# Attention block with keys and values formed once per head and head pairs, and the norms' weights and bias applied by VectorE in two combined steps

## Chip, cores and metric

The kernel runs on one core of one Trainium2 chip. The metric is the device time of one execution in microseconds (us). It is one long program of stages that follow each other with a barrier of all engines between them: a recurrent mixer, a gated feed-forward network (FFN), an attention block, a second FFN, a hybrid mixer and a mixture of experts. The change touches the attention block and the four layer norms that end the first four stages.

## What is computed

Cut from the reference: the attention block picks 128 of up to 512 earlier tokens for each query by a small indexer, and attends over them in 16 heads. Keys and values are both made from one latent of 128 numbers per token.

```
T=512  heads H=16  head width dh=64  latent 128  k_sel=128
proj  = h @ w_in                      # q, latent, q_idx, k_idx, w_idx
ckv   = rmsnorm(proj[..latent..])
score = sum_i w_idx[t,i] * relu(q_idx[t,i] . k_idx[s])      # 8 index heads, causal
sel   = top_k(score, 128)
q_lat[t,h] = q[t,h] @ w_uk[h]         # 64 -> 128
logits     = q_lat . ckv[s] / 8 + rel_bias[bucket(t-s), h]
p          = softmax over s in sel
o_lat[t,h] = sum_s p * ckv[s]
o[t,h]     = o_lat[t,h] @ w_uv[h]     # 128 -> 64
out        = o @ w_out
```

Each of the first two blocks ends its mixer and its FFN with `x = layernorm(ALPHA*x + (1+gate)*y) * g + b`.

## The kernel before, in words

Everything is fp32 with tokens in four tiles `t` of 128 rows. Each engine has its own instruction list, written out by hand, and semaphores order them; nothing is scheduled by a planner, so the order in the code is the order on the engine.

**Attention (`dsa`).** TensorE (PE) transposes `x`, then runs 17 projection jobs of 8 matmuls each (`project`, L1527): 4 for the latent, 1 for `ki`, 4 for `qi`, and after the indexer's scores 8 for the queries `qT`. ScalarE (ACT) copies each result out of PSUM. The scores (L1546) are 24 matmuls with a contraction of 64 rows, even index heads from rows 0 to 63 and odd ones from rows 64 to 127; ACT applies relu, VectorE (DVE) adds them up in `sel` (L1726, L1729), then finds the 128 largest of each row in 16 rounds per tile (L1739, L1740; 48 rounds of growing width) and turns `sel` into 0 or -1e30.

The loop over 16 heads then does for each head `h`: PE projects the query into the latent (`query_latents`, L1591), ACT copies it to `q_lat` (L1670); PE multiplies `q_lat` with `ckvT` for four causal tiles of 128, 256, 384 and 512 columns (L1601); DVE adds the bias (L1757), then adds `sel` and takes the row maximum in one instruction (L1759), and negates it (L1761); ACT takes the exponentials (L1687); PE transposes the ten 128x128 blocks of probabilities (`attend`, L1566); ACT copies them to `PT` (L1682); PE multiplies with `ckv` (`output`, L1576), ACT copies `o_lat` (L1692), PE applies `w_uv` (`project_output`, L1583), and DVE divides by the row sums (`finish`, L1747). The logits of head `h` stand on PE ahead of the transposes of head `h-1`. After the last head PE transposes the output (L1619) and multiplies it with `w_out` (L1626), 16 matmuls per token tile.

**Norms.** `deepnorm_rows` on DVE takes for each tile: gate times PSUM (L435), plus ALPHA times `x` (L436), statistics (L438), each in two halves; mean and variance (L439, L440); it waits for ACT's square root, takes the reciprocal (L442), and scales the tile in one instruction (L443). `affine_rows` on GpSimd (POOL) multiplies by `g` (L451) and adds `b` (L453), and SyncE (SP) stores the tile. It is used four times: in the mixer's last stage (tiles named `mixed_`), in both FFNs (`ffn_`) and in the attention block (`dsa_`, where `y` lies in `dsa_qT`).

Of the kernel before, what the change touches and what calls it, by code (L numbers as in the profile page):

```python
# [98 lines left out]
def swiglu(nc, phase, x_in, mod, w_in, w_out, ln_g, ln_b, ident_dram, x_out, next_cond, next_w, next_b, next_mod):  # L99
# [8 lines left out]
    with ExitStack() as ctx:  # L108
# [8 lines left out]
        with ExitStack() as down_ctx:  # L117
# [24 lines left out]
                   y_psum steps root var_done scaled g_done normed stored wi_highs wi_split wo_highs wo_split act_steps  # L142
# [15 lines left out]
        with nc.Block() as block:  # L158
# [54 lines left out]
            def _(pool):  # L213
# [6 lines left out]
                affine_rows(nc, pool, y, g, b, (s["v_loaded"], 16 * 3), s["scaled"], s["g_done"], s["normed"])  # L220
# [119 lines left out]
            def _(dve):  # L340
# [5 lines left out]
                for b in range(2):  # L346
                    nc.vector.memset(marks[:, 4 + b:5 + b], 0.0).then_inc(nstored[b], 16)
# [72 lines left out]
                for f in range(2, NF):  # L420
# [4 lines left out]
                deepnorm_rows(nc, dve, link, lambda t, j: bank[2 * t + j], s["y_psum"], x_again, gt, y, st, mv, rstd,  # L425
                              s["var_done"], s["root"], s["scaled"])


def deepnorm_rows(nc, dve, link, bank_of, y_psum, x, gt, y, st, mv, rstd, var_done, root, scaled):

    for t in range(NT):
# [11 lines left out]
        nc.vector.tensor_scalar(y[:, t, :], y[:, t, :], mv[:, t, 0:1], rstd[:, t:t + 1], ALU.subtract, ALU.mult).then_inc(scaled, 1)  # L443


def affine_rows(nc, pool, y, g, b, v_loaded, scaled, g_done, normed):

    pool.wait_ge(*v_loaded)
    for t in range(NT):
        pool.wait_ge(scaled, t + 1)  # L450
        nc.gpsimd.tensor_tensor(y[:, t, :], y[:, t, :], g[:, :], ALU.mult).then_inc(g_done, 1)  # L451
        pool.wait_ge(g_done, t + 1)
        nc.gpsimd.tensor_tensor(y[:, t, :], y[:, t, :], b[:, :], ALU.add).then_inc(normed, 1)  # L453

# [736 lines left out]
def rwkv_finish(nc, room, buf, Y, acc, x_in, mod, w, ln_g, ln_b, ident_dram, x_out):  # L1191
# [40 lines left out]
    scaled = room.sem("scaled")  # L1232
    g_done = room.sem("g_done")
# [4 lines left out]
    with nc.Block() as block:  # L1238
# [16 lines left out]
        def _(pool):  # L1255
# [3 lines left out]
            affine_rows(nc, pool, y, g, b, (v_loaded, 16 * 2), scaled, g_done, normed)  # L1259
# [51 lines left out]
        def _(dve):  # L1311
# [26 lines left out]
            deepnorm_rows(nc, dve, link, lambda t, j: bank[2 * (t % 3) + j], y_psum, x, gt, y, st, mv, rstd, var_done, root, scaled)  # L1338
# [43 lines left out]
def dsa(nc, x_in, mod, w, ln_g, ln_b, ident_dram, buckets_dram, causal_dram, rows_dram, skew_dram, x_out):  # L1382
# [8 lines left out]
    with ExitStack() as ctx:  # L1391
        room = Room(nc, ctx, "dsa")
        x = room.sb("x", [P, NT, D])
# [3 lines left out]
        y = qT[:, :, :].rearrange("p (t a) n -> p t (a n)", t=NT)  # L1397
        wq = room.sb("wq", [P, 2, KD * HALF])
# [45 lines left out]

        def ring(n):
            return wq[:, n, :].rearrange("p (k n) -> p k n", k=KD)

        with nc.Block() as block:

            @block.sync  # L1450
# [321 lines left out]
def by_dist_tile(L):  # L1772
    return L[0:HEADS, 0, 0:SKEW]
# [1255 lines left out]
```

## Time and profile before

| what | us |
|---|---|
| median of 3 runs | 3128.85 |
| lowest and highest | 3121.71, 3137.18 |
| the profiled execution's own time | 3123.55 |
| its span in the trace | 3121.8 |

The profiled execution is one run with a hardware trace. Its span goes from the first to the last instruction; its own time is 1.75 us more and is what the working is summed against. It lies 5.3 us under the median of the runs.

### The profile page before, as it was taken

To read this page: it belongs to the slowest core of one execution; us is meant where nothing else is said; L and a number is where in the kernel's file an instruction comes from. 1 tells how busy PE (TensorE), PEld (TensorE's weight loads), DVE (VectorE), ACT (ScalarE), POOL (GpSimd) and SP (SyncE) were. 2 spreads that over 40 slices of the span, in tenths; PEclk is the share of its full clock that TensorE was granted. 3 is DMA by queue.
4 is the path that set the end of the run, shared out by engine and by line. 5 is a ranking of instruction groups with operands and counts; after the bars stand their busy time and mean duration, and the time that the engine had idled before them with its cause. 6 is when DMAs were issued, how large, how long until landed. Compare 5 with 4: busy or idle time off the path is not lost. (4 is left out here: it accounts for less than half of the span.)

```text
span 3121.8 us, 41213 instructions
## 1 busy us (share of the span) xinstructions
PE 2637.2 (84%) x16425; PEld 1923.8 (62%) x16425; DVE 1983.2 (64%) x2679; ACT 924.7 (30%) x999; POOL 488.7 (16%) x246
## 2 busy tenths in 40 slices
PE   5999888849999589776799993998894599999991
PEld 3444888337778444443577783896543488888870
DVE  7581666767663528433677536786623599999983
ACT  2101111112220021440222101343200477777761
POOL 0000000120000310002000003000000256656642
PEclk8998999979999899998899996999996699999995
DMA  4210121256652281000765433231306399999963
GB/s 177 80 71 33 57 71 71 109 177 185 184 161 101 103 265 54 1 1 28 223 186 174 134 104 130 81 95 54 135 14 254 113 359 364 369 362 356 357 246 124
DMA packets 248302, 481.05 MB, mean 154 GB/s; under 512 B 31734, under 2 KB 195086, under 8 KB 232809
## 3 DMA queue, kind: packets, MB, share of 16 engines
q1 hardware_dynamic: 227256, 453.59, 41.5%
q0 software_dynamic: 14368, 23.79, 2.2%
q10 hardware_dynamic: 6546, 1.79, 0.3%
q8 instruction: 98, 1.61, 0.2%
q14 instruction: 34, 0.28, 0.0%
HBM read 472.70 MB, written 36.85 MB: 163 GB/s over the span
## 5 line engine op out<-in xcount | busy, mean ns | idle before, releaser
L49 PE MATMUL ffn_bank<-ffn_xT_high,ffn_wi_high 128*128 128x512 f32 x704 | 281.1, 399 | 5.2 <-ACT ffn_xT L309 3.2
L51 PE MATMUL ffn_bank<-ffn_xT_high,ffn_wi_low 128*128 128x512 f32 x704 | 275.2, 391 | 0.0
L50 PE MATMUL ffn_bank<-ffn_xT_low,ffn_wi_high 128*128 128x512 f32 x704 | 275.2, 391 | 0.0
L303 ACT CAST ffn_wi_high<-ffn_wi 128x2048 fp32r<-128x2048 f32 x44 | 84.0, 1910 | 382.0 <-DMA ffn_wi<-in_ffn_w_in 302.0
L383 DVE SCALAR_TENSOR_TENSOR ffn_nsum<-ffn_nw,ffn_cond,ffn_nsum 128x256 f32<-128x256 f32 x336 | 162.9, 485 | 12.0
L49 PEld LDWEIGHTS ffn_bank<-ffn_xT_high,ffn_wi_high 128*128 128x128 f32 x704 | 132.8, 189 | 53.4 <-issue 16.6
L2735 POOL DMA_INDIRECT expert_rows<-exp_ys,exp_to_row x32 | 155.8, 4870 | 45.1 <-issue 44.3
L43 DVE TENSOR_TENSOR moe_g_low<-moe_g,exp_g_high 128x4096 fp32r<-128x4096 f32 x32 | 141.6, 4425 | 30.2 <-ACT exp_g_high L2810 30.2
L51 PEld LDWEIGHTS ffn_bank<-ffn_xT_high,ffn_wi_low 128*128 128x128 f32 x704 | 132.8, 189 | 28.6
L43 DVE TENSOR_TENSOR moe_u_low<-moe_u,exp_u_high 128x4096 fp32r<-128x4096 f32 x32 | 141.6, 4425 | 13.1 <-ACT exp_u_high L2810 13.1
L2810 ACT CAST exp_g_high<-moe_g 128x4096 fp32r<-128x4096 f32 x32 | 116.5, 3641 | 112.5 <-PE exp_p_g L51 83.2
L50 PEld LDWEIGHTS ffn_bank<-ffn_xT_low,ffn_wi_high 128*128 128x128 f32 x704 | 132.9, 189 | 26.2
L451 POOL TENSOR_TENSOR ffn_y<-ffn_y,ffn_g 128x1024 f32<-128x1024 f32 x8 | 18.8, 2354 | 816.4 <-DVE ffn_y L443 816.4
L43 DVE TENSOR_TENSOR ffn_wi_low<-ffn_wi,ffn_wi_high 128x2048 fp32r<-128x2048 f32 x44 | 100.8, 2291 | 70.2 <-ACT ffn_wi_high L303 70.2
L43 DVE TENSOR_TENSOR moe_d_low<-moe_d,exp_d_high 128x4096 fp32r<-128x4096 f32 x32 | 141.4, 4418 | 0.0
L49 PE MATMUL ffn_bank<-ffn_wo_high,ffn_act_high 128*128 128x512 f32 x352 | 137.4, 390 | 3.1 <-DVE ffn_wo_low L43 3.1
L51 PE MATMUL ffn_bank<-ffn_wo_high,ffn_act_low 128*128 128x512 f32 x352 | 137.0, 389 | 0.0
L50 PE MATMUL ffn_bank<-ffn_wo_low,ffn_act_high 128*128 128x512 f32 x352 | 136.9, 389 | 0.0
L2810 ACT CAST exp_d_high<-moe_d 128x4096 fp32r<-128x4096 f32 x32 | 116.5, 3641 | 1.9 <-DMA moe_d<-in_w_e_down 1.9
L2719 POOL COPY exp_from_row<-exp_rows 128x2 int32 (+1 forms) x30 | 113.7, 3791 | 19.5 <-PE exp_p_x L2764 19.3
L2810 ACT CAST exp_u_high<-moe_u 128x4096 fp32r<-128x4096 f32 x32 | 116.2, 3632 | 0.0
L360 DVE CAST ffn_wo_high<-ffn_wo 128x1024 fp32r<-128x1024 f32 x44 | 30.5, 693 | 130.7 <-DMA ffn_wo<-in_ffn_w_out 130.7
(599 smaller groups left out, 6172.3 us busy)
## 6 DMA issues: line engine op xcount, KB each, us to landing
moe_g<-in_w_e_gate SPq DMA_DIRECT2D x32, 2048.0 KB, 10.0
moe_u<-in_w_e_up SPq DMA_DIRECT2D x32, 2048.0 KB, 9.8
moe_d<-in_w_e_down SPq DMA_DIRECT2D x32, 2048.0 KB, 9.7
ffn_wi<-in_ffn_w_in SPq DMA_DIRECT2D x88, 512.0 KB, 5.2
ffn_nw<-in_ada_w SPq DMA_DIRECT2D x24, 1024.0 KB
ffn_nw<-in_w_ada SPq DMA_DIRECT2D x24, 1024.0 KB
ffn_wo<-in_ffn_w_out SPq DMA_DIRECT2D x44, 512.0 KB, 3.3
hyb_wb<-in_w_in SPq DMA_DIRECT2D x20, 1024.0 KB, 5.8
```

The costliest lines, as they stand in the source:

```text
L43: return engine.tensor_tensor(low, x, high.bitcast(F32), ALU.subtract)
L49: nc.tensor.matmul(out, w[0], x[0], start=start, stop=False, **kw)
L50: nc.tensor.matmul(out, w[0], x[1], start=False, stop=False, **kw)
L51: return nc.tensor.matmul(out, w[1], x[0], start=False, stop=stop, **kw)
L303: nc.scalar.copy(wi_high[h][:, :, :, :], wi[h][:, :, :, :]).then_inc(s["wi_highs"], 1)
L360: nc.vector.tensor_copy(wo_high[slot][:, :], wo[slot][:, :]).then_inc(s["wo_highs"], 1)
L383: nc.vector.scalar_tensor_tensor(out=total, in0=nw[:, b, k, :], scalar=cond[:, k:k + 1], in1=total, op0=ALU.mult, op1=ALU.add).then_inc(s[ ...
L451: nc.gpsimd.tensor_tensor(y[:, t, :], y[:, t, :], g[:, :], ALU.mult).then_inc(g_done, 1)
L2719: nc.gpsimd.tensor_copy(from_row[h][:, :, :], rows[:, bass.ds(n, 1), :]).then_inc(s["from_copied"], 1)
L2735: nc.gpsimd.indirect_dma_start(ys_dram, bass.IndirectOffsetOnAxis(ap=to_row[h][:, 0, 1:2].bitcast(U32), axis=0), ys[h][:, :], None, bounds ...
L2810: nc.scalar.copy(flat(high_of(name, h)[:, :, :]), flat(raw[name][h][:, :, :])).then_inc(s[f"{name}_high"], 1)
```

## The change

**Attention.** Once, before the queries' projection, PE transposes `w_uk` (8 transposes) and forms the keys `kT` of all heads, two heads per matmul (8 matmuls, scaled by 1/8 as ACT copies them), and the values `v` of all heads (8 matmuls); ACT copies the 18 results. Scores are now formed between the projections, one pair of index heads after each. The loop runs over 8 pairs of heads. For a pair, PE first writes `sel` into PSUM with a single-pass matmul against the identity (both in fp32r, `ident_r` and `sel_r`), then adds query times key with a contraction of 64 rows, one head from rows 0 to 63 and the other from rows 64 to 127, into the same place. DVE takes logits plus bias and the maximum in one instruction, straight from PSUM. The 20 transposes stand in five rounds over banks 6 and 7, copied by ACT (three) and DVE (two); the output is probabilities times `v`, 20 matmuls of 64 columns. There is no `q_lat`, no `o_lat`, and no separate `w_uv` step. `x` is read again from memory at the end, since `v` takes its place.

**Norms.** `affine_rows` is gone. DVE does `(y - mean) * g` and then `* rstd + b`, two instructions over 128x1024, where it had one.

```diff
-        nc.vector.tensor_scalar(y[:, t, :], y[:, t, :], mv[:, t, 0:1], rstd[:, t:t + 1], ALU.subtract, ALU.mult).then_inc(scaled, 1)
-def affine_rows(nc, pool, y, g, b, v_loaded, scaled, g_done, normed):
-        nc.gpsimd.tensor_tensor(y[:, t, :], y[:, t, :], g[:, :], ALU.mult).then_inc(g_done, 1)
-        nc.gpsimd.tensor_tensor(y[:, t, :], y[:, t, :], b[:, :], ALU.add).then_inc(normed, 1)
+        link(nc.vector.scalar_tensor_tensor(out=y[:, t, :], in0=y[:, t, :], scalar=mv[:, t, 0:1], in1=g[:, :], op0=ALU.subtract, op1=ALU.mult))
+        nc.vector.scalar_tensor_tensor(out=y[:, t, :], in0=y[:, t, :], scalar=rstd[:, t:t + 1], in1=b[:, :], op0=ALU.mult, op1=ALU.add).then_inc(normed, 1)
...
+        GROUPS = [[(0, 2), (0, 0)], [(1, 2), (1, 0)], [(0, 3)], [(1, 3)], [(0, 1), (1, 1)]]
+        ROUNDS = [[(0, 0)], [(0, 1), (0, 3)], [(1, 0)], [(1, 1), (1, 3)], [(0, 2), (1, 2)]]
+        ACT_ROUNDS, DVE_ROUNDS = (0, 2, 4), (1, 3)
...
+                sp.wait_ge(s["o_psum"], KD)
+                for t in range(NT):
+                    sp.dma_start(x_again[:, t, :], x_in[t * P:(t + 1) * P, :]).then_inc(s["x_again_loaded"], 16)
...
+                for q in range(KD):
+                    out = prepared(2 + q)
+                    nc.tensor.matmul(out[:, :], w_ukT[:, q, :], ckvT[:, :], start=True, stop=True).then_inc(s["prep_psum"], 1)
+                for t in range(NT):
+                    for j in range(2):
+                        out = prepared(10 + 2 * t + j)
+                        nc.tensor.matmul(out[:, :], ckvT[:, t * P:(t + 1) * P], w_uv_cols[:, j * HALF:(j + 1) * HALF],
+                                         start=True, stop=True).then_inc(s["prep_psum"], 1)
...
+                    for t in (2, 0, 3):
+                        for e in range(2):
+                            if t:
+                                free(e if t == 2 else 2 + e)
+                            masked(e, t)
+                        for e in range(2):
+                            last = scored(e, t)
+                            if t != 2:
+                                last.then_inc(s["l_psum"], 1)
+                    free(4)
+                    nc.tensor.matmul(bank[4][:, :].rearrange("p (e n) -> p e n", e=2), ident_r[:, :],
+                                     sel_r[:, OFF[1]:OFF[1] + NK[1]].rearrange("p (a n) -> p a n", a=1).broadcast_to([P, 2, NK[1]]),
+                                     start=True, stop=False, skip_group_check=True)
+                    scored(0, 1).then_inc(s["l_first"], 1)
+                    pe.wait_ge(s["l_first"], q + 1)
+                    scored(1, 1).then_inc(s["l_psum"], 1)
...
+                logits(0)
+                for q in range(KD):
+                    if q + 1 < KD:
+                        logits(q + 1)
+                    transposed(q, 0)
+                    transposed(q, 1)
+                    if q:
+                        output(q - 1, 0)
+                    transposed(q, 2)
+                    transposed(q, 3)
+                    if q:
+                        output(q - 1, 1)
+                    transposed(q, 4)
...
+                    for e, t in GROUPS[group]:
+                        col = COLUMN[e, t]
+                        ins = link(nc.vector.tensor_tensor_reduce(L[:, q % 2, e, OFF[t]:OFF[t] + NK[t]], logits_at(e, t), bias[:, 2 * q + e, T - NK[t]:T],
+                                                                  1.0, TAKEN, ALU.add, ALU.max, nmax[:, q % 2, col:col + 1]))
```

Here is what stands on PE for one head in the middle of the loop before (the first four rows are the logits of the next head).

```order
L1601 MATMUL dsa_bank<-dsa_ckvT,dsa_q_lat 128x128
L1601 MATMUL dsa_bank<-dsa_ckvT,dsa_q_lat 128x256
L1601 MATMUL dsa_bank<-dsa_ckvT,dsa_q_lat 128x384
L1601 MATMUL dsa_bank<-dsa_ckvT,dsa_q_lat 128x512
L1591 MATMUL dsa_bank<-dsa_qT,dsa_w_uk 128x512
L1566 MATMUL dsa_bank<-dsa_ident,dsa_L 128x128 x10
L1576 MATMUL dsa_bank<-dsa_PT,dsa_ckv 128x512
L1576 MATMUL dsa_bank<-dsa_PT,dsa_ckv 128x384
L1576 MATMUL dsa_bank<-dsa_PT,dsa_ckv 128x256
L1576 MATMUL dsa_bank<-dsa_PT,dsa_ckv 128x128
L1583 MATMUL dsa_bank<-dsa_w_uv,dsa_o_lat 128x64 x4
```

And here what stands on PE for one pair of heads in the middle of the loop of the changed kernel, up to the second round of transposes.

```order
L1611 MATMUL dsa_bank<-dsa_sel_r,dsa_ident_r 128x384 x2
L1616 MATMUL dsa_bank<-dsa_kT,dsa_qT 128x384 x2
L1611 MATMUL dsa_bank<-dsa_sel_r,dsa_ident_r 128x128 x2
L1616 MATMUL dsa_bank<-dsa_kT,dsa_qT 128x128 x2
L1611 MATMUL dsa_bank<-dsa_sel_r,dsa_ident_r 128x512 x2
L1616 MATMUL dsa_bank<-dsa_kT,dsa_qT 128x512 x2
L1629 MATMUL dsa_bank<-dsa_sel_r,dsa_ident_r 128x512
L1616 MATMUL dsa_bank<-dsa_kT,dsa_qT 128x256 x2
L1646 MATMUL dsa_bank<-dsa_ident,dsa_L 128x128 x8
L1659 MATMUL dsa_bank<-dsa_v,dsa_PT 128x64 x10
```

Another 8 transposes, 10 output matmuls and 4 transposes follow. The 46 instructions of two heads have become 55: 15 make the logits, 20 are transposes and 20 the output. The steps through `q_lat` and `o_lat` are no longer there.

For the norms, this is the end of a tile and the start of the next on DVE before, here in the mixer (`mixed_`).

```order
L439 BN_AGGR mixed_mv<-mixed_st 128x2
L440 TENSOR_SCALAR mixed_mv<-mixed_mv 128x1
L442 RECIPROCAL mixed_rstd<-mixed_rstd 128x1
L443 TENSOR_SCALAR mixed_y<-mixed_y,mixed_mv,mixed_rstd 128x1024
L435 TENSOR_TENSOR mixed_y<-mixed_bank,mixed_gt 128x512
```

And the same place in the changed kernel.

```order
L440 BN_AGGR mixed_mv<-mixed_st 128x2
L441 TENSOR_SCALAR mixed_mv<-mixed_mv 128x1
L443 RECIPROCAL mixed_rstd<-mixed_rstd 128x1
L444 SCALAR_TENSOR_TENSOR mixed_y<-mixed_y,mixed_mv,mixed_g 128x1024
L445 SCALAR_TENSOR_TENSOR mixed_y<-mixed_y,mixed_rstd,mixed_b 128x1024
L436 TENSOR_TENSOR mixed_y<-mixed_bank,mixed_gt 128x512
```

One instruction has become two, and the two of POOL per tile are gone.

## Rows read from the trace of the kernel before

**Rows 1.** The page's first line: the span.
```profile
span 3121.8 us, 41213 instructions
```

**Rows 2.** Windows; columns: length, PE, PEld, DVE, ACT, POOL busy, PE clock, DMA.
```profile
1152.00:1229.00 77.00, 73.38 (x180) 31.70 (x178) 70.47 (x169) 15.88 (x31) 0.00 (x0) 1.00 0.14 51
1229.00:1396.00 167.00, 129.63 (x563) 80.16 (x563) 77.13 (x291) 75.59 (x207) 0.00 (x0) 0.96 0.03 14
1250.00:1300.00 50.00, 39.20 (x179) 24.62 (x178) 23.08 (x87) 23.52 (x65) 0.00 (x0) 1.00 0.00 1
```

**Rows 3.** Timeline of PE, one head in the loop's middle; columns: start, length.
```profile
1307.47 1.10 PE L1583 MATMUL dsa_bank<-dsa_w_uv,dsa_o_lat 128*128 128x64 f32 x8 [0.68 <-ACT dsa_o_lat L1692]
1308.41 2.38 PE L1601 MATMUL dsa_bank<-dsa_ckvT,dsa_q_lat 128*128 128x128 f32 x8
1310.72 1.12 PE L1591 MATMUL dsa_bank<-dsa_qT,dsa_w_uk 64*128 64x512 f32 x2
1311.77 1.31 PE L1566 MATMUL dsa_bank<-dsa_ident,dsa_L 128*128 128x128 f32 x10
1314.57 2.39 PE L1576 MATMUL dsa_bank<-dsa_PT,dsa_ckv 128*128 128x512 f32 x8 [1.49 <-issue]
1317.64 1.10 PE L1583 MATMUL dsa_bank<-dsa_w_uv,dsa_o_lat 128*128 128x64 f32 x8 [0.68 <-ACT dsa_o_lat L1692]
```

**Rows 4.** Timeline of PE around the projections, the loop's start and its end.
```profile
1121.00 27.63 PE L1527 MATMUL dsa_bank<-dsa_hT,dsa_wq 128*128 128x512 f32 x64
...
1166.96 55.20 PE L1527 MATMUL dsa_bank<-dsa_hT,dsa_wq 128*128 128x512 f32 x128
1222.85 1.12 PE L1591 MATMUL dsa_bank<-dsa_qT,dsa_w_uk 64*128 64x512 f32 x2 [0.69 <-ACT dsa_qT L1643]
...
1396.93 1.09 PE L1619 MATMUL dsa_bank<-dsa_ident,dsa_hT 128*128 128x128 f32 x8 [0.59 <-DVE dsa_hT L1747]
```

**Rows 5.** Tile `dsa_L`: ns min/median/max, first and last start, forms.
```profile
L1757 DVE TENSOR_TENSOR dsa_L<-dsa_bank,dsa_bias x64: 279/486/692, 1230.3 to 1383.2; 128x128 f32<-128x128 f32 x16, 128x256 f32<-128x256 f32 x16, 128x384 f32<-128x384 f32 x16, 128x512 f32<-128x512 f32 x16
L1759 DVE CUSTOM_DVE_ANT_0 dsa_L<-dsa_L,dsa_sel x64: 291/492/694, 1230.7 to 1383.9; 128x128 f32<-128x128 f32 x16, 128x256 f32<-128x256 f32 x16, 128x384 f32<-128x384 f32 x16, 128x512 f32<-128x512 f32 x16
L1687 ACT ACTIVATE dsa_L<-dsa_L,dsa_nmax x64: 401/564/722, 1231.2 to 1385.8; 128x128 f32<-128x128 f32 x16, 128x256 f32<-128x256 f32 x16, 128x384 f32<-128x384 f32 x16, 128x512 f32<-128x512 f32 x16
```

**Rows 6.** Groups of 1250 to 1350, forms apart: count, busy us, mean ns.
```profile
L1682 ACT COPY dsa_PT<-dsa_bank 128x512 f32<-128x512 f32 x20 | 10.7, 588 | 6.4 <-PE dsa_bank L1566 6.4
```

**Rows 7.** The indexer's first two score matmuls: timeline, and source line (ns min/median/max).
```profile
1149.32 0.70 PE L1546 MATMUL dsa_bank<-dsa_ki,dsa_qi 64*128 64x256 f32 x4 [0.25 <-ACT dsa_qi L1643]
L1546 PE MATMUL dsa_bank<-dsa_ki,dsa_qi x4: 376/428/480, 1149.3 to 1149.6; 64*128 64x256 f32 x4
```

**Rows 8.** Timeline of PE in the FFN: two fp32r matmuls that follow each other.
```profile
1048.73 0.39 PE L49 MATMUL ffn_bank<-ffn_wo_high,ffn_act_high 128*128 128x512 f32 x1
1048.96 0.39 PE L50 MATMUL ffn_bank<-ffn_wo_low,ffn_act_high 128*128 128x512 f32 x1
```

**Rows 9.** The mixer's norm: source line L436 (ns), then timeline of DVE and POOL.
```profile
L436 DVE SCALAR_TENSOR_TENSOR mixed_y<-rwkv_BT,mixed_y x8: 691/1271/2407, 609.0 to 639.3; 128x512 f32<-128x512 f32 x8
634.00 0.81 DVE L443 TENSOR_SCALAR mixed_y<-mixed_y,mixed_mv,mixed_rstd 128x1024 f32<-128x1024 f32 x1
642.16 0.81 DVE L443 TENSOR_SCALAR mixed_y<-mixed_y,mixed_mv,mixed_rstd 128x1024 f32<-128x1024 f32 x1
645.47 2.34 POOL L453 TENSOR_TENSOR mixed_y<-mixed_y,mixed_b 128x1024 f32<-128x1024 f32 x1
```

**Rows 10.** Source line L2971, the last stage: ns min/median/max.
```profile
L2971 DVE SCALAR_TENSOR_TENSOR comb_yj<-comb_yj,moe_weight x4: 1274/1282/1285, 3089.1 to 3106.6; 128x1024 f32<-128x1024 f32 x4
```

**Rows 11.** Timelines: DVE in the attention's norm; SP and DVE before the FFN's norm.
```profile
1447.04 0.16 DVE L442 RECIPROCAL dsa_rstd<-dsa_rstd 128x1 f32<-128x1 f32 x1 [31.61 <-ACT dsa_rstd L1700]
1039.33 2.24 SPq L206 DMA_DIRECT2D ffn_x_again<-x  x4
1048.18 0.69 DVE L435 TENSOR_TENSOR ffn_y<-ffn_bank,ffn_gt 128x512 f32<-128x512 f32 x1 [3.14 <-DMA ffn_x_again<-x]
```

More of the change, by code:

```diff
@@ L1580, in project_output @@
-                def project_output(h):
-                    pe.wait_ge(s["olat_done"], h + 1)
-                    for t in range(NT):
-                        last = nc.tensor.matmul(bank[7][:, 256 + t * HD:256 + (t + 1) * HD], o_lat[:, h % 2, t * P:(t + 1) * P], w_uv[:, h, :],
-                                                start=True, stop=True)
-                    last.then_inc(s["o_psum"], 1)
-                def query_latents(h):
-                    q, rows = h // 2, slice(HD * (h % 2), HD * (h % 2 + 1))
-                    if h >= 3:
-                        pe.wait_ge(s["olat_done"], h - 2)
-                    nc.tensor.matmul(bank[4][:, :], w_uk[rows, q, :], qT[rows, q, :], start=True, stop=True).then_inc(s["qlat_psum"], 1)
@@ L1612, in _ @@
-                pe.wait_ge(s["o_done"], HEADS)
+                for n in range(2):
+                    out = prepared(n)
+                    for q in range(4):
+                        last = nc.tensor.transpose(out[:, q * P:(q + 1) * P], w_uk[:, 4 * n + q, :], ident[:, :])
+                    last.then_inc(s["prep_psum"], 1)
+                scores(3)
+                for q in range(KD):
+                    out = prepared(2 + q)
+                    pe.wait_ge(s["prep_done"], 1 + q // 4)
+                    nc.tensor.matmul(out[:, :], w_ukT[:, q, :], ckvT[:, :], start=True, stop=True).then_inc(s["prep_psum"], 1)
@@ new lines, in _ @@
+                for group in range(5):
+                    exponentials(0, group)
+                for q in range(KD):
+                    more = q + 1 < KD
+                    if more:
+                        exponentials(q + 1, 0)
+                    evict(q, 0)
+                    if more:
+                        exponentials(q + 1, 1)
+                        exponentials(q + 1, 2)
+                    evict(q, 2)
+                    if more:
+                        exponentials(q + 1, 3)
+                    evict(q, 4)
+                    if more:
+                        exponentials(q + 1, 4)
@@ new lines, in _ @@
+                dve.wait_ge(s["bias_loaded"], 16 * HEADS)
+                for group in range(5):
+                    maxima(0, group)
+                for q in range(KD):
+                    more = q + 1 < KD
+                    if more:
+                        maxima(q + 1, 0)
+                        maxima(q + 1, 1)
+                    evict(q, 1)
+                    if more:
+                        maxima(q + 1, 2)
+                        maxima(q + 1, 3)
+                    evict(q, 3)
+                    if more:
+                        maxima(q + 1, 4)
+                    if q:
+                        finish(q - 1)
```

352 lines of the change are left out of this document (188 added, 164 removed).

## The prediction

> **What bounds the kernel now.** I first read the page for the span [rows 1], then windows over the attention block, then timelines of one engine at a time. The stages are cut apart by barriers, so a gain in one is a gain in the whole, and only the attention block and the four norms need a sum.
>
> In the attention block three stretches follow each other. Up to the loop, two chains run side by side: PE's query projections, which end about 1222, and DVE's search for the largest scores, which ends when DVE first touches the logits at 1230.3 [rows 4, 5]. The window 1152 to 1229 shows both busy, 73.4 and 70.5 of 77 us [rows 2]. DVE ends last, by about 8 us. Then come 16 heads up to 1396.9, when PE transposes the output [rows 4]: 166.6 us from DVE's first logits. In it no engine is full: PE 129.6 of 167, DVE 77.1, ACT 75.6 [rows 2]. One head takes 10.17 us, from one `project_output` at 1307.47 to the next at 1317.64 [rows 3]. Start to start, PE spends in it: `project_output` 0.94, logits 2.31, `query_latents` 1.05, the ten transposes 1.3, a wait of 1.5 for ACT's copies, `output` 2.4, and 0.7 for `o_lat`. So the loop is a ring PE, ACT, PE, ACT, with PE the longest member. Last comes the output projection with the norm, where DVE waits 31.6 us for ACT's square root, which stands behind the copies of all tiles [rows 11], and then works through the tiles by itself.
>
> In every norm DVE sets the end, and GpSimd's two operations follow the last tile. From one tile's L443 to the next is 8.16 us, and from the last L443 at 642.16 to the end of L453 (645.47 + 2.34) is 5.65 us [rows 9].
>
> **The norms.** L436 takes 0.69 us alone, but its median is 1.27 and its maximum 2.41 while GpSimd works [rows 9]. Per tile one instance takes about 2.35 and one 1.27; with GpSimd silent both take 0.69, which saves 1.66 + 0.58 = 2.24 us. L443, a slot of 0.73, goes, and two operations over 128x1024 come; the nearest row is L2971 at 1.28 us each [rows 10], so +1.8 with the gaps. A tile takes 8.16 - 2.24 + 1.8 = 7.7 us. Three periods save 1.4, and the end after the last reciprocal is 2.6 in place of 5.65, 3.05 saved. That is 4.4 a norm, 18 us for four. Bounds: if DVE's new pair cost twice the row (2.56 each), a tile would take 10.4, three periods would lose 6.7 and the end would gain 0.4, a loss of 6.3 a norm; nothing in the rows points there. At best the pair costs what L443 costs per element, and a norm gains 8 us. I take 18 in all. This holds in the attention block too: DVE starts at 1447, after ACT's square root, and the last tile's matmuls are finished before DVE gets to it.
>
> **Ahead of the loop.** The projections of `qi` take 27.6 us for four [rows 4], 6.87 each, and stay. The scores are taken apart into four groups of six between them. They are paced by relu and DVE, and PE can run on to the next projection while the last two of a group are being taken, about 1 us in each. New are the transposes of `w_uk` (8 at 0.115 each, by the ten in 1.31 [rows 3], of which some 0.16 is the last one's run-out) and ACT's two copies ahead of the last group. I let PE reach the point after the scores at 1166, as at 1166.96 before [rows 4]. Then come 16 matmuls of 128x512 for keys and values: 128 records in 55.2 us are 64 matmuls [rows 4], 0.86 each, and ACT's copy of 0.59 [rows 6] fits between two banks; 14 us. The queries' 55 us follow, so PE is ready at 1166 + 14 + 55 + 0.7 = 1235.7. DVE's search ends about 1229. So the eight us in which PE used to be early are used up, PE takes the lead, and the loop starts at 1235.7. Bounds: 1230 if the scores lose their bubbles, 1240 if each group fills and drains by itself.
>
> **One pair of heads on PE.** A fp32 matmul goes in two records; 512 columns take 0.86, so a column takes 1.67 ns.
> - Masks: fp32r, one record. Two 128x512 start 0.23 apart [rows 8], so 0.44 ns a column; short ones take no less than a transpose's 0.115. Two each of 384, 128 and 512 and one of 512: 1.2 us.
> - Query times key: 2560 columns, 4.27 us one after the other. But the two heads lie in the two row halves. The indexer's first two score matmuls, 256 columns each in opposite halves, took 0.70 us for four records; one after the other they need three times 0.213 (256 columns at 0.83 ns a record) plus a last record of at least 0.376, or 1.02 [rows 7]. So the halves work side by side. Then 384 costs 0.64, 128 costs 0.35 (its four weight loads), 512 costs 0.86, and the two of 256, which share a bank and wait for each other, 1.15. Together 3.0.
> - Going from 128 rows to 64 and back: `query_latents` starts 2.31 after the logits, of which 2.13 are columns, and lasts 1.05 until the transposes, of which 0.86 are columns [rows 3]. I take 0.3 for both ways; there are four such excursions in a pair, 1.2 us.
> - 20 transposes at 0.115: 2.3 us.
> - 20 output matmuls of 64 columns: `project_output` has the same shapes and takes 0.94 for four [rows 3], so 4.7 us.
>
> The sum is 1.2 + 3.0 + 1.2 + 2.3 + 4.7 = 12.4 us, against 20.3 for two heads before.
>
> The Trainium skill, "TensorEngine Tiling (Array Packing)", in Key Properties and in Gotcha 1, speaks against this part: changing the tiling mode drains the engine, and two row tiles can't use one PSUM bank at the same time. The rows agree with the first, at about 0.3 us for both ways, and by that the pair stays at 12.4; for the second no run here has two halves in one bank. It gives no figure for either. Were the halves to wait for each other in different banks too, the pair would be 14.0, the first rival below.
>
> **Who waits in the pair.** DVE: eight maxima of at most 0.69 plus 0.1 [rows 5] (its PSUM source costs no more, L1757 has the same length), five negations, two copies, one division: about 7.7 us. ACT: eight exponentials of at most 0.72 [rows 5] and three copies of 0.59 [rows 6]: at most 7.6. Both fit under 12.4. I went through the order: transposes of round 2 need ACT's copy of round 0, which is out 0.8 us after round 0, while PE does round 1 and half an output (2.35 us); round 4 is behind the second half likewise; DVE's maxima of the last group end after round 3 but the next pair's logits (5.4 us on PE) lie between. So in the steady state PE waits for nobody. Not hidden: in the first pair no output fills the rounds (2.3 us), before the last pair's transposes there are no logits (1.9 us), before the last output 0.9, the last division 1. The loop takes 8 x 12.4 + 6 = 105 us, so PE transposes the output at 1235.7 + 105 = 1341, 56 us earlier than 1396.9.
>
> The second load of `x` is issued when the last output is done. In the FFN the same four loads, issued from 1039.33, were waited for until 1048.18 [rows 11], 8.9 us. In the attention block the first product is due about 9 us after that point (division 0.6, transposes and copy 1.7, eight matmuls at 0.86), and behind it DVE has its 31 us wait for the square root. It costs nothing; without that cover, about 1 us.
>
> **Sum.** 3123.55 - 56 - 18 = 3049.5. The profiled execution lies 5.3 us under the median of its runs, and the changed kernel's runs may lie on either side; I give 3051.
>
> **The rivals.**
> - *The halves don't help* (fp32 with two records, a mask in the same bank just before): 4.27 + 0.4 in place of 3.0 is 1.6 a pair, 13 us: 3064. Against it stands the 0.70 us; for it, that this was one instance at an empty engine. 0.14.
> - *The hand-offs show.* If each copy between rounds on one bank were waited for, three times 0.8 and a last 0.9 are 3.3 a pair, 26 us: 3077. For it, the loop before loses 2.2 us a head to just this; against it, the output halves put between. 0.14.
> - *PE packs tighter*: the small output matmuls overlap with the transposes or the loop starts at 1230: 10 us less, 3040. 0.08.
> - *The norms give nothing*, because the two new operations cost 1.1 us more per tile than the row: 3069. 0.07.
> - *Slower than before*: the PE clock. In the loop's middle it was granted at 1.00, which is 2.4 GHz [rows 2]; the pair has more short transposes and 64-column matmuls than a head had. At 1.2 GHz a pair takes 25 us, the loop 206, ends at 1441, 45 us late, and with the norms' 18 the kernel is at 3152. It decides from 21.6 us a pair on. Against it: PE is fuller than before, when 78% busy kept it at 1.00. 0.03.
> - *No effect*, the loop being held elsewhere, by DVE's bias loads or a queue I missed: 3129. 0.02.
>
> **How the numbers follow.** The forecast has 0.52, with a range of its own from 3036 to 3062 (a pair of 11.5 to 13 us, a start 4 us to either side). What a measurement can tell from no change here is about 0.5%, 15.6 us, so faster begins below 3113. All cases but the last two are there: 0.95, with 0.02 for the same and 0.03 slower. The range takes in the better case and the hand-offs: 3028 to 3083.
>
> **What the changed profile would show.** Right: PE over 90% busy in the loop and a pair every 12 to 13 us; records of L1616 in pairs that start together; DVE and ACT about 60% busy; the first logits on PE at about 1236 after the last query projection, with DVE idle before them; L437 at 0.69 throughout and L444, L445 at 1.28. Wrong: idle time on PE ahead of L1646 or L1659 released by ACT or DVE; L1616 at full serial length; a clock under 1.00 in the loop; DVE still in L1830 when PE is ready; or L444 over 2 us.

## The result, and the profile after

| what | us |
|---|---|
| before, median of 4 runs | 3127.07 (3121.71 to 3137.18) |
| after, median of 4 runs | 3051.98 (3046.11 to 3063.65) |
| ratio | 0.9767, interval 0.9746 to 0.9788 |
| spans of the two profiled executions | 3121.8 and 3049.6 |

The kernel is 2.3% faster; 3051 was predicted. The spans differ by 72.2 us, where the sum had 74. To see where they lie, take the load of the identity that opens each stage (timeline of SyncE, kernel after; the rows are the starts of the mixer's last stage, the FFN, the attention block and the second FFN):

```profile
545.09 0.33 SPq L1231 DMA_DIRECT2D mixed_ident<-in_ident  x1
646.12 0.34 SPq L172 DMA_DIRECT2D ffn_ident<-in_ident  x1
1076.99 0.33 SPq L1463 DMA_DIRECT2D dsa_ident<-in_ident  x1
1413.26 0.33 SPq L172 DMA_DIRECT2D ffn_ident<-in_ident  x1
```

The same four rows of the kernel before:

```profile
549.14 0.33 SPq L1242 DMA_DIRECT2D mixed_ident<-in_ident  x1
652.17 0.34 SPq L172 DMA_DIRECT2D ffn_ident<-in_ident  x1
1087.76 0.33 SPq L1452 DMA_DIRECT2D dsa_ident<-in_ident  x1
1481.57 0.33 SPq L172 DMA_DIRECT2D ffn_ident<-in_ident  x1
```

From row to row the stages are shorter by 2.0 (mixer), 4.7 (FFN) and 57.5 (attention), and the second FFN, measured likewise, by 5.5. The other 2.4 lie in stages that the change doesn't touch: 4.0 gained ahead of the first row and 1.6 lost behind the second FFN. The first row lies at 549.1 in the one profile of the kernel before, and between 541.1 and 545.9 in the 13 others of this study, all with the same code ahead of it. So that part is most likely variation; with one profile of before it isn't shown. Times of after inside the attention block are best read against the stage's own start, 10.8 us earlier than before.

**The loop's start.** Timeline of PE (start, length; in brackets idle time and releaser), to be read against [rows 4]:

```profile
1155.70 7.43 PE L1588 MATMUL dsa_bank<-dsa_ckvT,dsa_L 128*128 128x512 f32 x16
1162.96 7.42 PE L1593 MATMUL dsa_bank<-dsa_w_uv,dsa_ckvT 128*128 128x512 f32 x16
1170.21 55.10 PE L1540 MATMUL dsa_bank<-dsa_hT,dsa_wq 128*128 128x512 f32 x128
1226.00 0.62 PE L1611 MATMUL dsa_bank<-dsa_sel_r,dsa_ident_r 128*128 128x384 f32 x2 [0.69 <-ACT dsa_qT L1711]
```

and DVE's first row of the loop:

```profile
1228.39 0.56 DVE L1839 CUSTOM_DVE_ANT_0 dsa_L<-dsa_bank,dsa_bias 128x384 f32<-128x384 f32 x1 [8.81 <-PE dsa_bank L1616]
```

Keys and values take 14.5 us, the queries 55.1, and the first mask starts at 1226.0. Brought to this trace, the prediction's 1235.7 is 1224.9. DVE had finished at 1219.6 and waits 8.8 us: the lead has passed to PE.

**A pair.** Timeline of PE, seventh passage of the loop:

```profile
1303.02 0.60 PE L1611 MATMUL dsa_bank<-dsa_sel_r,dsa_ident_r 128*128 128x384 f32 x2
1303.55 0.92 PE L1616 MATMUL dsa_bank<-dsa_kT,dsa_qT 64*128 64x384 f32 x4
1304.39 0.44 PE L1611 MATMUL dsa_bank<-dsa_sel_r,dsa_ident_r 128*128 128x128 f32 x2
1304.76 0.49 PE L1616 MATMUL dsa_bank<-dsa_kT,dsa_qT 64*128 64x128 f32 x4
1305.18 0.74 PE L1611 MATMUL dsa_bank<-dsa_sel_r,dsa_ident_r 128*128 128x512 f32 x2
1305.85 1.13 PE L1616 MATMUL dsa_bank<-dsa_kT,dsa_qT 64*128 64x512 f32 x4
1306.91 0.49 PE L1629 MATMUL dsa_bank<-dsa_sel_r,dsa_ident_r 128*128 128x512 f32 x1
1307.34 1.45 PE L1616 MATMUL dsa_bank<-dsa_kT,dsa_qT 64*128 64x256 f32 x4
1308.72 1.09 PE L1646 MATMUL dsa_bank<-dsa_ident,dsa_L 128*128 128x128 f32 x8
1309.64 2.34 PE L1659 MATMUL dsa_bank<-dsa_v,dsa_PT 128*128 128x64 f32 x20
1311.82 1.04 PE L1646 MATMUL dsa_bank<-dsa_ident,dsa_L 128*128 128x128 f32 x8
1312.70 2.34 PE L1659 MATMUL dsa_bank<-dsa_v,dsa_PT 128*128 128x64 f32 x20
1314.88 0.61 PE L1646 MATMUL dsa_bank<-dsa_ident,dsa_L 128*128 128x128 f32 x4
```

No row has idle time ahead of it. Start to start, masks and products take 5.70 us, transposes 2.17 (0.93, 0.88 and 0.36), outputs 4.36: 12.23 a pair, in place of 20.3 for two heads [rows 3]. The window of the loop's middle (columns as in [rows 2]):

```profile
1254.10:1303.00 48.90, 48.67 (x335) 36.32 (x334) 26.95 (x121) 25.50 (x76) 0.00 (x0) 1.00 0.01 1
```

PE is busy there for 99.5% at a granted clock of 1.00, 2.4 GHz; DVE 55% and ACT 52%.

The loop before, against which this is measured, had not run at full clock throughout. At 1230.78, behind a wait of 2.64 us for DVE (L1757), PE starts the second head's logits (L1601), and the granted clock is low there:

```profile
1231.00:1246.00 15.00, 12.95 (x28) 6.11 (x27) 8.00 (x30) 6.92 (x21) 0.00 (x0) 0.54 0.22 90
```

From 1230.78 to the first `project_output` at 1246.45 are 15.7 us. The same instructions take 11.7 in the kernel with the norms alone (1224.28 to 1235.95, clock 0.86). So some 4 us of the 57.5 are clock that the profile of before had lost, and no work saved.

**The loop's end and the output projection.**

```profile
1317.16 1.09 PE L1646 MATMUL dsa_bank<-dsa_ident,dsa_L 128*128 128x128 f32 x8 [1.67 <-ACT dsa_L L1756]
...
1324.61 4.68 PE L1659 MATMUL dsa_bank<-dsa_v,dsa_PT 128*128 128x64 f32 x40 [0.68 <-ACT dsa_PT L1763]
1330.14 1.97 PE L1687 MATMUL dsa_bank<-dsa_ident,dsa_hT 128*128 128x128 f32 x8 [0.85 <-DVE dsa_hT L1856]
1332.79 16.05 PE L1694 MATMUL dsa_bank<-dsa_wq,dsa_bias 128*128 128x512 f32 x32 [0.68 <-ACT dsa_bias L1785]
```

The output's transposes start at 1330.14; 1341, less 10.8, is 1330.2. But they take 1.97 us where they took 1.09 [rows 4], and the first projection 16.05 where the later three take 14.00. In the window the granted clock is half.

```profile
1330.00:1336.00 6.00, 5.18 (x12) 3.08 (x13) 0.09 (x1) 1.17 (x2) 0.00 (x0) 0.51 0.89 333
```

**The norms.** Source lines in the mixer, ns min/median/max, to be read against [rows 9, 10]:

```profile
L437 DVE SCALAR_TENSOR_TENSOR mixed_y<-rwkv_BT,mixed_y x8: 691/692/693, 607.7 to 637.2; 128x512 f32<-128x512 f32 x8
L444 DVE SCALAR_TENSOR_TENSOR mixed_y<-mixed_y,mixed_mv,mixed_g x4: 1284/1285/1285, 616.3 to 639.5; 128x1024 f32<-128x1024 f32 x4
```

L445 has the same length. A tile takes (639.5 - 616.3) / 3 = 7.73 us in place of 8.16, and the last ends 2.6 us after its L444 begins.

### The profile page after: what moved, and what is told of

Its sections match the earlier page's. It is cut to its first block and busy times, and to the rows that moved or that the text cites. A ratio compares the mean times of both kernels' runs of the same rounds, so it can differ in the third digit from the quotient of the medians.

```text
span 3049.6 us, 41307 instructions
## 1 busy us (share of the span) xinstructions
PE 2620.9 (86%) x16553; PEld 1921.2 (63%) x16553; DVE 1961.9 (64%) x2648; ACT 912.1 (30%) x961; POOL 407.7 (13%) x214
## 5 line engine op out<-in xcount | busy, mean ns | idle before, releaser
L2916 ACT CAST exp_g_high<-moe_g 128x4096 fp32r<-128x4096 f32 x32 | 116.7, 3646 | 110.8 <-PE exp_p_g L51 81.4
L49 PE MATMUL exp_p_g<-exp_g_high,exp_xT_high 128*128 128x512 f32 x256 | 105.5, 412 | 8.3 <-DVE exp_xT_low L43 8.3
```

The lines of the kernel that those rows point to most:

```text
L49: nc.tensor.matmul(out, w[0], x[0], start=start, stop=False, **kw)
L2916: nc.scalar.copy(flat(high_of(name, h)[:, :, :]), flat(raw[name][h][:, :, :])).then_inc(s[f"{name}_high"], 1)
```

## The experiments

Twelve kernels, each with its ratio to the kernel before. "Stage" is the attention block's length from its first load to the next stage's: before 393.8, after 336.3.

**The norms alone**: the diff's norm part applied to the kernel before. 

> The kernel before with the change to the four norms alone. By the prediction each norm gives 4.4 us, 18 in all: ratio 0.994, about 3109 us, with L436's successor at 0.69 us throughout and a tile every 7.7 us. If the whole gain of the change lay in the attention block (the rival that the norms give nothing) the ratio would be 1.000.

Measured: 3105.98 us, ratio 0.9931 (0.9909 to 0.9953). L437 is 0.69 throughout (691/692/693 ns in the mixer), also where POOL used to be beside it. The mixer's stage is 2.2 shorter, the FFNs' 4.4 and 6.1. The attention block's is 2.9 longer (396.7), although its norm is shorter by the same 4.4 as in the changed kernel (83.2 us from the output's transposes to the next stage, 2.9 of them to the clock, against 84.6). Ahead of the loop the granted clock fell here while PE formed the indexer's scores, whose code is unchanged; they took 24.8 us in place of 17.6 [rows 4, 7]:

```profile
1130.00:1160.00 30.00, 28.86 (x64) 12.65 (x62) 13.30 (x24) 11.52 (x24) 2.65 (x6) 0.66 0.44 165
```

That the norms give nothing is excluded, by the ratio and by each stage's own norm.

**The attention alone**: the changed kernel with the former norms. 

> The changed kernel with the norms as they were before, on VectorE and GpSimd. By the prediction's terms, less the 3 us that the cooled PE clock took at the output projection, 53 us of gain: ratio 0.983, about 3074 us, and the loop over pairs still takes 104 us from the first mask to the output's transposes. If the two parts helped each other (a norm that is freed only by the new attention), the two ratios would not add up to 0.977.

Measured: 3061.95 us, ratio 0.9794 (0.9773 to 0.9815); stage 338.2, 55.6 less than before. The time is 12 us under the 3074 expected; in the profile 8.1 us more are gained ahead of the mixer's last stage, which the change doesn't touch. Loop from 1230.74 to the output's transposes at 1334.89, 104.2 us. The two gains, 0.69% and 2.06%, add up to 2.75%, where the whole has 2.33%; the 0.42 between them is a little more than three intervals of 0.2 allow together (0.37), so the ratios leave open whether the parts influence each other. In the traces the loop (104.2 and 104.1 us) and the norm in the attention block (4.4 us shorter) have the length that they have in the whole. Here 1.8 us lie between the output's transposes and the first projection and not 2.65: the clock hadn't fallen.

**Both heads in one row half.** 

> The changed kernel, with both heads of a pair taking rows 0 to 63 of queries and keys, so that the two heads' matmuls can't lie side by side; the odd heads' logits are thereby those of the even ones. If the side-by-side halves are what makes query times key 3.7 us with its excursions, the pair goes from 12.2 to between 13.5 and 13.9 us and the kernel is 10 to 13 us slower than the changed one: about 3064. If the two heads' matmuls never overlapped and the short time has another cause, the pair stays at 12.2 and the time at 3052.

```diff
-                        rows = slice(HD * e, HD * (e + 1))
+                        rows = slice(0, HD)
```

Measured: 3064.46 us, ratio 0.9811 (0.9779 to 0.9844); a pair 13.94 us. Timeline of PE:

```profile
1263.94 1.55 PE L1616 MATMUL dsa_bank<-dsa_kT,dsa_qT 64*128 64x384 f32 x4
...
1265.79 0.71 PE L1616 MATMUL dsa_bank<-dsa_kT,dsa_qT 64*128 64x128 f32 x4
...
1267.10 1.98 PE L1616 MATMUL dsa_bank<-dsa_kT,dsa_qT 64*128 64x512 f32 x4
...
1269.44 1.45 PE L1616 MATMUL dsa_bank<-dsa_kT,dsa_qT 64*128 64x256 f32 x4
```

The three shapes that lay side by side take 0.63, 0.22 and 0.85 us more, 1.71 in all; the last, whose two products wait for each other anyway, takes the same 1.45. So the halves do work side by side, and that is worth 8 x 1.71 = 13.7 us. The first rival is excluded as the state of the changed kernel, and its price was right.

**Outputs behind the fifth round.** 

> The changed kernel with both output halves behind the fifth round of transposes, so that nothing covers the copies between rounds on one bank. The first pair, which has no outputs, lost 2.3 us to this. If the covered hand-offs are what keeps PE full, seven more pairs lose 2.3 us each: pair 14.5 us, kernel about 3068. If the copies would be in time anyway, nothing changes. The rival of the prediction (3.3 us a pair) would give 3075.

```diff
-                    transposed(q, 0)
-                    transposed(q, 1)
-                    if q:
-                        output(q - 1, 0)
-                    transposed(q, 2)
-                    transposed(q, 3)
-                    if q:
-                        output(q - 1, 1)
-                    transposed(q, 4)
+                    for n in range(5):
+                        transposed(q, n)
+                    if q:
+                        output(q - 1, 0)
+                        output(q - 1, 1)
```

Measured: 3087.97 us (3075.3 to 3099.5), ratio 0.9862 (0.9836 to 0.9887), 20 us more than the 3068 expected and 13 more than the rival's 3075. Windows, one pair each from 1241.0 on:

```profile
1241.00:1255.60 14.60, 12.73 (x86) 9.10 (x85) 6.52 (x33) 8.01 (x26) 0.00 (x0) 1.00 0.01 1
1255.60:1272.80 17.20, 15.33 (x86) 11.69 (x85) 6.65 (x30) 6.24 (x19) 0.00 (x0) 0.84 0.00 1
1272.80:1297.20 24.40, 23.32 (x86) 16.60 (x85) 6.64 (x30) 6.24 (x19) 0.00 (x0) 0.50 0.00 0
```

The first pair takes the expected 14.6: the uncovered copies cost 2.4. Then the granted clock falls to half, 1.2 GHz, and a pair takes up to 24.4. That is my slower rival (25 us a pair), in a loop that has two gaps of 0.33 and 1.48 us in each pair.

**The same with the gaps filled.** 

> The kernel with the outputs behind the fifth round, with 2 and 11 transposes of the identity, that nobody reads, in the two gaps that PE has in a pair. There the pair took 14.6 us while the clock was 1.00, and 17 to 24 after it had fallen. If the gaps make the clock fall, every pair now takes 14.6 to 14.8 and the kernel 3052 + 7 * 2.4 = about 3069, 19 under the unfilled 3088. If it is the mix of short operations that makes the clock fall, it falls here too.

```diff
+                    if n in (2, 4):
+                        if q >= 2:
+                            pe.wait_ge(s["o_done"], q - 1)
+                        for _ in range({2: 2, 4: 11}[n]):
+                            nc.tensor.transpose(bank[5][:, 0:P], ident[:, :], ident[:, :])
```

Measured: 3070.16 us (3062.8 to 3073.13), ratio 0.9806 (0.9789 to 0.9823). Each of the five pairs from 1243.7 to 1316.9 takes 14.63 us, and the clock stays at 1.00 up to 1331:

```profile
1272.00:1301.00 29.00, 28.10 (x192) 20.84 (x192) 13.30 (x60) 12.48 (x38) 0.00 (x0) 1.00 0.00 1
```

PE does 13 transposes more in a pair and the kernel is 18 us faster. The short operations are all still there, so it was the gaps. Behind the last pair, where nothing is filled, the clock fell here too (0.79 from 1331 to 1350). The outputs between the rounds are worth two things: 2.4 us a pair at full clock, and the full clock.

**Two of sixteen matmuls for keys and values.** 

> The changed kernel with 2 of the 16 matmuls for keys and values; ScalarE still makes all 16 copies, which leaves keys and values wrong. PE saves 12.7 us ahead of the loop. By the prediction VectorE's search, which ended at 1219.6 with PE's first mask at 1226.0, then becomes the last: the loop starts 6 us earlier and not 12.7, and PE waits for the search at its first mask. Kernel about 3046. If PE alone set the start, 12.7 us are gained (3039); if the search had set it all along, nothing.

Measured: 3059.05 us (3053.74 to 3060.38), ratio 0.9772 (0.9751 to 0.9793). PE's first mask:

```profile
1218.20 0.98 PE L1606 MATMUL dsa_bank<-dsa_sel_r,dsa_ident_r 128*128 128x384 f32 x2 [7.12 <-DVE dsa_sel_r L1826]
```

PE now waits 7.1 us for the search. From the projection of `ki` to the first mask are 116.7 us; in every other profile of the new attention they are 123.0, as from 1103.03 to 1226.00 in the changed kernel. So 6.3 are gained and not 12.7, which is what the search's end allows. The time is no better all the same. Behind the 7 us of idle PE the clock was low: the first mask takes 0.98 in place of 0.62 and the first pair's masks and products 8.8 in place of 5.7, which is 3.1 of the 6.3. The rest went at the loop's end, where the clock fell again (0.60 from 1310 to 1330): from the last pair's transposes to the output's are 21.8 us in place of 13.0. The kernels with the masks first and with the unfilled gaps lost as much there with all 16 matmuls in place, so this loss isn't put down to the missing ones. The stage is 344.1.

**Gaps at the loop's end filled.** 

> The changed kernel with transposes of the identity, that nobody reads, in the three places at the end of the loop where PE has nothing to do (8, 5 and 6 of them). In the changed kernel's trace the clock fell to 0.50 there and the first output projection took 15.9 in place of 13.8 us. If the clock falls because PE has gaps there, it stays at 1.00, the transposes take 1.1 and the first projection 14.0, and the stage is up to 3 us shorter. If the reload of x, which runs in the same stretch, slows PE, the first projection stays at 16.

```diff
+                def idle_work(out, count):
+                    for _ in range(count):
+                        nc.tensor.transpose(out[:, 0:P], ident[:, :], ident[:, :])
...
+                    if q == KD - 1 and n == 0:
+                        pe.wait_ge(s["pt_act"], 3 * q)
+                        idle_work(bank[6], 8)
...
+                pe.wait_ge(s["l_taken"], 5 * KD)
+                idle_work(bank[0], 5)
...
+                idle_work(bank[0], 6)
```

Measured: 3046.54 us (3044.19 to 3052.11), ratio 0.9735 (0.9715 to 0.9755).

```profile
1334.19 1.09 PE L1697 MATMUL dsa_bank<-dsa_ident,dsa_hT 128*128 128x128 f32 x8 [0.19 <-DVE dsa_hT L1866]
1336.01 14.00 PE L1704 MATMUL dsa_bank<-dsa_wq,dsa_bias 128*128 128x512 f32 x32 [0.73 <-ACT dsa_bias L1795]
```

The transposes take 1.09 and the projection 14.00 again, though `x` is read from memory in just this stretch (328 GB/s from 1334 to 1338). So the reload isn't what slowed PE. That the filling held the clock this one kernel doesn't prove: attention alone, one row half, roots early and GpSimd beside have the same gaps, and theirs didn't fall either.

**Roots early.** 

> The changed kernel with ScalarE's square root of tile t in the attention's norm placed behind the copies of tile t+1, in place of all four behind the copies of tile 3. VectorE then does tiles 0 to 2 (7.7 us each) under PE's projections (15.6 us each), and behind PE's last matmul at 1395.5 only half a tile, the root and the two new operations are left, 6 to 7 us: the norm ends about 1402 and not at 1409.2, 7 us less, kernel about 3045. The rival is that ScalarE has to load its table anew at each change between copy and square root (1.3 us each) in PE's path, 8 us, and nothing is gained.

```diff
+                    if t:
+                        square_root(t - 1)
+                square_root(NT - 1)
-                for t in range(NT):
-                    act.wait_ge(s["var_done"], t + 1)
-                    nc.scalar.activation(rstd[:, t:t + 1], mv[:, t, 1:2], ACT.Sqrt).then_inc(s["root"], 1)
```

Measured: 3040.36 us (3034.01 to 3053.83), ratio 0.9724 (0.9699 to 0.9748). In DVE's timeline the wait of 31.6 us ahead of the first reciprocal [rows 11] is gone, and behind PE's last matmul only the last tile's norm is left, up to 1401.8:

```profile
1352.38 0.17 DVE L443 RECIPROCAL dsa_rstd<-dsa_rstd 128x1 f32<-128x1 f32 x1 [0.41 <-ACT dsa_rstd L1783]
```

From the output's transposes to the next stage are 72.5 us; in the kernel with filled gaps, whose clock is the same, 80.3: 7.8 gained. ACT's table was loaded once (1.28 us at 1350.86) and not at each change.

**Masks first.** 

> The changed kernel with the masks of two groups written before the products of both, so that PE goes from 128 rows to 64 and back twice in a pair, and once more in the last group, in place of four times. By the prediction's 0.3 us for both ways, 0.6 us a pair are saved, 5 us in all: pair 11.6 us, kernel about 3047. If going back and forth costs nothing of its own and the time lies in the columns alone, the pair stays at 12.2. If waiting for the last group's bank earlier (VectorE hasn't read it yet) costs more than that, the pair gets longer.

```diff
+                    for e in range(2):
+                        free(e)
+                        masked(e, 2)
+                        masked(e, 0)
+                    for t in (2, 0):
+                        for e in range(2):
+                            last = scored(e, t)
...
+                    for e in range(2):
+                        free(2 + e)
+                        masked(e, 3)
+                    free(4)
...
+                    for e in range(2):
+                        scored(e, 3).then_inc(s["l_psum"], 1)
```

Measured: 3049.13 us (3036.53 to 3052.96), ratio 0.9734 (0.9711 to 0.9757). A pair has two excursions in place of four (the expectation's words count one too many, its 0.6 us doesn't) and takes 11.43 us, 0.80 less: 0.4 for each. An excursion is a change from 128 rows to 64, a change from fp32r to fp32, and the start of a new run of matmuls; which of the three costs the 0.4 this kernel doesn't separate. But at the end the clock fell earlier than before (0.59 from 1313 on), the last outputs took 8.80 in place of 4.68, and the stage is 341.6. In this kernel the masks of 384 and 128 lie in one bank, and the second opens a sum of its own before the first has been added to. The Trainium skill, "PSUM — Partial Sum Buffer", The four PSUM rules, says that the first matmul of a sum clears the written marks of the whole bank, so that the next matmul of the open sum overwrites it. By that rule the tiles of 384 keys lose their mask here, and no trace shows it; in the next kernel only the first of the two masks opens a sum. The time doesn't hang on it: a pair takes 11.43 in both.

**Masks first, roots early and filled gaps together.** 

> The changed kernel with the masks written first, the roots early and the filled gaps together; of the two masks that share a bank only the first opens the bank's sum, so that both are kept. From the runs so far: 0.8 us a pair from the masks (6.4), 7 from the roots, and a clock that stays at 1.00 to the end of the loop. Attention stage 336.3 - 6.4 - 7 - 2.9 = 320, kernel about 3035, ratio 0.970. If filling doesn't hold the clock where the masks are written first (there it fell at 1313, ahead of the last outputs), the stage takes 5 to 8 us more.

```diff
-                        nc.tensor.matmul(logits_at(e, t), ident_r[:, :], sel_r[:, OFF[t]:OFF[t] + NK[t]], start=True, stop=False,
+                        nc.tensor.matmul(logits_at(e, t), ident_r[:, :], sel_r[:, OFF[t]:OFF[t] + NK[t]], start=(t != 0), stop=False,
```

Measured: 3029.88 us (3029.07 to 3038.72), ratio 0.9682 (0.9668 to 0.9696); stage 322.0. Masks and products take 4.90 us of a pair of 11.43:

```profile
1278.59 0.77 PE L1611 MATMUL dsa_bank<-dsa_sel_r,dsa_ident_r 128*128 128x384 f32 x4
1279.29 1.14 PE L1616 MATMUL dsa_bank<-dsa_kT,dsa_qT 64*128 64x384 f32 x8
1280.35 0.74 PE L1611 MATMUL dsa_bank<-dsa_sel_r,dsa_ident_r 128*128 128x512 f32 x2
1280.92 0.40 PE L1632 MATMUL dsa_bank<-dsa_sel_r,dsa_ident_r 128*128 128x512 f32 x1
1281.25 2.31 PE L1616 MATMUL dsa_bank<-dsa_kT,dsa_qT 64*128 64x512 f32 x8
```

**The same without the filling.** 

> The same without the transposes that fill the gaps. If the gaps at the end of the loop let the clock fall, as in the run with the masks first, the last outputs take up to 12 us more and the first output projection 2 us more, and the median lies 3 to 10 us above that of the filled kernel. If the clock falls by chance and not by the gaps, the two are equal.

Measured: 3040.73 us (3028.86 to 3046.45), ratio 0.971 (0.9688 to 0.9732); stage 331.2. Windows of the end of the loop, first without the filling:

```profile
1305.00:1320.00 15.00, 13.02 (x75) 12.38 (x74) 3.80 (x13) 3.02 (x8) 0.00 (x0) 0.67 0.01 2
```

and with it:

```profile
1312.00:1328.00 16.00, 15.00 (x132) 14.16 (x131) 4.01 (x12) 3.33 (x8) 0.00 (x0) 1.00 0.01 2
```

In these two profiles the stage is 9.3 us shorter with the filling. The medians lie 11 us apart, but the lowest runs agree (3028.86 and 3029.07) and the two intervals overlap by a little (to 0.9696, from 0.9688), so the times alone don't show the gain. With gaps the clock may fall and may not; what decides it stays open.

**GpSimd beside the norm.** 

> The changed kernel with two operations of 128x1024 on GpSimd behind each of the first three tiles of the mixer's norm, on buffers that nobody needs any more. They stand where the two of the old norm stood. If GpSimd's traffic is what made L436 2.35 and 1.27 us long, L437 does the same here and a tile takes 7.7 + 2.2 = 9.9 us: the mixer's last stage is 6.7 us longer, 107.7 in place of 101.0, the kernel about 3059. If the length came from GpSimd and VectorE working on the same tile y, nothing changes: 3052.

```diff
+            for t in range(NT - 1):
+                pool.wait_ge(normed, t + 1)
+                nc.gpsimd.tensor_tensor(V[:, t, :], g[:, :], b[:, :], ALU.mult)
+                nc.gpsimd.tensor_tensor(G[:, t, :], g[:, :], b[:, :], ALU.add)
```

Timelines of POOL, at work on tiles of its own, and of DVE:

```profile
614.95 2.35 POOL L1252 TENSOR_TENSOR rwkv_V<-mixed_g,mixed_b 128x1024 f32<-128x1024 f32 x1 [62.82 <-DVE mixed_y L445]
...
614.70 0.69 DVE L436 TENSOR_TENSOR mixed_y<-mixed_bank,mixed_gt 128x512 f32<-128x512 f32 x1
615.41 2.44 DVE L437 SCALAR_TENSOR_TENSOR mixed_y<-rwkv_BT,mixed_y 128x512 f32<-128x512 f32 x1
617.88 0.69 DVE L439 BATCH_NORM_STATS2 mixed_st<-mixed_y 128x6 f32<-128x512 f32 x1
...
619.34 1.27 DVE L437 SCALAR_TENSOR_TENSOR mixed_y<-rwkv_BT,mixed_y 128x512 f32<-128x512 f32 x1
```

L437 has its two old lengths back, 2.44 and 1.27. L436, which has one input in PSUM, and L439, which has one input, stay at 0.69 between them. A tile takes 10.0 us. From the norm's first reciprocal (611.98) to the next stage's first load (649.10) are 37.1 us, in the changed kernel 616.12 to 646.12, 30.0; the stage is 5.6 longer, since it began its norm earlier. The Trainium skill, "SBUF — State Buffer", SBUF: two separate sides, has the rule: a DVE operation with two inputs from SBUF and a GpSimd operation that reads SBUF exclude each other for a whole instruction. The trace agrees: the first L437 ends at 617.85, 0.55 behind the end of POOL's first operation (617.30), and the second at 620.61, 0.55 behind that of its second (L1253, 617.26 to 620.06). The kernel's time, 3051.74 us in four runs (to 3067.7), ratio 0.9767 (0.974 to 0.9794), doesn't show the 6 us: the interval is 17 us wide, and the first stages of the profiled run were 2.7 us shorter than in the changed kernel.

## Why the prediction was right

- **The loop's start.** Right. 14.5 us for keys and values (14), 55.1 for the queries, first mask within 1.1 us of its place. That PE takes the lead from DVE was shown by leaving out 12.7 us of PE's work, of which 6.3 came back.
- **The pair.** 12.23 against 12.4, but three terms were off and made up for each other; that is in part luck. An excursion from the masks to the products and back costs 0.4 and not 0.3 (masks first), so 1.6 in place of 1.2; the outputs 4.36 in place of 4.7 and the transposes 2.17 in place of 2.3. The outputs stand in runs of ten matmuls, and I took their price from runs of four; that a longer run pays its start once is argued and not shown. What is left, 12.23 - 1.6 - 4.36 - 2.17 = 4.1, stands against 4.2 for masks and products.
- **Side by side.** Right, and right in size: 1.6 a pair was said for its absence, 1.71 measured.
- **Who waits.** Right in the steady state. First pair 2.3 and last pair 1.9 as said: 4.47 against 2.17 us for the rounds, 2.28 against 0.36 ahead of the last pair's first. Hand-offs, were they shown, cost 2.4 a pair at full clock; the rival had 3.3.
- **The slower rival.** Right to be there, wrong in what goes with it. I argued with the length of the operations ("more short transposes and 64-column matmuls") and took PE's fullness as a help. The runs show the same short operations at full clock with the gaps filled, and at half clock with two gaps of together 1.8 us a pair. My argument from the busy share was no better: at 78% [rows 2] the loop before kept 1.00, and at 87% the loop with the outputs last did not. What tells these two apart stays open.
- **The reload of x.** Right, it costs nothing: DVE's first operation of the norm waited for PE and not for it.
- **Behind the loop.** The step that failed. I took the output projection as unchanged; the transposes and the first projection took 2.9 us more at the lower clock. So the stage gained 57.5 and not 60.4. Nor did I see that the 166.6 us I measured the loop against held some 4 us of low clock of their own.
- **The norms.** 4.4 each was said; the stages give 2.0, 4.7, 5.5 and, in the attention block, 84.6 - 83.1 + 2.9 = 4.4 from the output's transposes to the stage's end (clock taken out). From the mixer's first reciprocal to the next stage it is 34.8 - 30.0 = 4.8; what is missing in its stage lies ahead of the norm. The mechanism, two operations of DVE that become long beside GpSimd, was shown from both sides: by taking GpSimd away and by putting it back on other tiles.
- **The sum.** 3049.5 for the profiled execution against 3051.3. The missing 2.9 behind the loop and 1.4 of the norms are partly made up by the 2.4 of the untouched stages, and the loop's 56 hold only against a profile of before that had lost clock, so part of this closeness is luck. How large such luck can be the kernel without the norms' part shows: 64 us of gain by its median, where its stage has 56.

## What to carry to other kernels

When a loop waits in a ring of two engines, put work of the neighbouring turn between a hand-off's two ends, and count twice what it saves: the wait, and the PE clock that the wait may cost. Before removing PE work ahead of a wait for another engine, ask who arrives last; 12.7 us less work brought the first mask 6.3 us forward, and 3.1 of these went at once, since the idle PE came back at half clock. Where PE must wait, work that nobody reads can be worth its place: 18 us with two gaps in each pair, and 9 at the loop's end in one pair of profiles. And a cheap look at the order of a waiting engine (ACT's square roots behind all copies) gave 7.8 us, more than a tenth of the whole change.

## What the runs showed of the hardware

- The granted clock fell to half (1.2 GHz) in the loop with two gaps a pair and not with these filled. Around single gaps of 0.7 to 1.7 us at the loop's end it fell in some profiles (the changed kernel, the masks first, two of sixteen matmuls, all three unfilled) and not in others with the same gaps (attention alone, one row half, roots early, GpSimd beside). The unchanged scores ran at 1.00 in the profile of before and at 0.66 in that of the norms alone.
- Leaving fp32r masks over 128 rows for fp32 products over 64 rows and coming back costs PE 0.4 us; what share the change of rows has isn't separated.
- Two heads' fp32 products in opposite row halves and different banks overlap fully: 512 columns each take 1.13 us together and 1.98 one after the other.
- A custom DVE operation that adds and takes the maximum costs the same from PSUM (128 columns 0.29 us, 512 columns 0.69) as it did from SBUF [rows 5].
